# Joins between the stages of a two-layer decoder trunk: chunk before tile, projection copies between the steps of the norm, squares in PSUM

## What is computed

```
for i in range(2):
    x = x + (attention, retention)[i](rmsnorm(x, norm_mix[i]))
    a = rmsnorm(x, norm_ffn[i]) @ ffn_w_in[i];  gate, up = a[..., :2816], a[..., 2816:]
    x = x + (silu(conv(gate)) * up) @ ffn_w_out[i]
    x = x + sigmoid(rmsnorm(x, norm_pl[i]) @ pl_w_gate[i]) * (p[i] @ pl_w_proj[i])
return rmsnorm(x, norm_final)
```

## Time and profile before

| | |
|---|---|
| median of 3 runs | 1542.73 us (1542.4 to 1547.37) |
| profiled execution | 1548.81 us, of which the span of its instructions is 1547.0 |
| PE busy | 1514.2 us (98%), mean granted clock 0.993 |
| DVE, ACT, POOL busy | 777.3, 634.4, 822.8 us (50, 41, 53%) |
| DMA | 137.77 MB, mean 89 GB/s |

### The profile page before, as it was taken

The page is one execution under the profiler, slowest core; times in us unless marked ns, Lnnn a source line. Parts: engine busy times, 40 slices in busy tenths (PEclk is TensorE's granted clock), DMA queues, the critical chain, the costliest instruction groups (busy, mean ns, idle before and its releaser), DMA issues.

```text
span 1547.0 us, 20602 instructions
## 1 busy us (share of the span) xinstructions
PE 1514.2 (98%) x6874; PEld 1254.2 (81%) x6874; DVE 777.3 (50%) x1201; ACT 634.4 (41%) x955; POOL 822.8 (53%) x1014
## 2 busy tenths in 40 slices
PE   8999999999999999999999999999999999999996
PEld 5888887788888888887888888888788888888874
DVE  6898996555555411257343433423755555511155
ACT  6777875433323322244343423424533323322232
POOL 5343343766666655465445354453566666655551
PEclk9999999999999999999999999999999999999998
DMA  4111111222222322223222122221222222333221
GB/s 168 61 61 61 41 55 55 99 97 104 95 95 95 139 94 93 68 96 129 89 70 102 61 95 81 81 99 64 95 89 102 95 95 95 115 113 106 73 82 55
DMA packets 37192, 137.77 MB, mean 89 GB/s; under 512 B 4128, under 2 KB 4256, under 8 KB 37024
## 3 DMA queue, kind: packets, MB, share of 16 engines
q1 hardware_dynamic: 36576, 134.61, 25.0%
q10 hardware_dynamic: 576, 2.62, 0.5%
HBM read 135.12 MB, written 2.10 MB: 89 GB/s over the span
## 4 chain that ended last, share of the span: by engine, by line
PE 78%; issue 11%; POOL 7%; DVE 2%; ACT 0%; DMA 0%; DVEq 0%; POOLq 0%; SPq 0%; ACTq 0%
PE bank L339 24%; PE bank L343 24%; PE bank L342 24%; POOL wl L310 7%; PE bank L601 2%; PE bank L606 2%; PE bank L605 2%; DVE sumsq L723 0%; DVE xl L729 0%; PE bank L665 0%; DVE x L1094 0%; DMA raw<-in_w 0%; DVE sumsq_l L709 0%; DVE x L951 0%; DVE gated L948 0%
## 5 line engine op out<-in xcount | busy, mean ns | idle before, releaser
L310 POOL TENSOR_TENSOR wl<-raw,wh 128x256 fp32r<-128x256 f32 x1008 | 820.7, 846 | 690.8 <-ACT wh L1101 690.5
L339 PE MATMUL bank<-xh,wh 128*128 128x512 f32 x1280 | 503.7, 393 | 5.9 <-DVE xl L729 4.4
L342 PE MATMUL bank<-xl,wh 128*128 128x512 f32 x1280 | 500.4, 391 | 0.0
L343 PE MATMUL bank<-xh,wl 128*128 128x512 f32 x1280 | 500.4, 391 | 0.0
L1101 ACT ACTIVATE wh<-raw 128x1024 fp32r<-128x1024 f32 (+1 forms) x236 | 260.4, 1104 | 527.7 <-PE bank L339 470.4
L339 PEld LDWEIGHTS bank<-xh,wh 128*128 128x128 f32 x1280 | 241.6, 189 | 59.8 <-DVE xl L729 8.3
L343 PEld LDWEIGHTS bank<-xh,wl 128*128 128x128 f32 x1280 | 241.5, 189 | 51.0
L342 PEld LDWEIGHTS bank<-xl,wh 128*128 128x128 f32 x1280 | 241.7, 189 | 48.9
L743 DVE TENSOR_TENSOR x<-x,bank 128x512 f32<-128x512 f32 x56 | 38.4, 686 | 245.7 <-PE bank L343 245.6
L342 PE MATMUL bank<-yl,wh 128*128 128x512 f32 x352 | 137.0, 389 | 0.0
L343 PE MATMUL bank<-yh,wl 128*128 128x512 f32 x352 | 137.0, 389 | 0.0
(11 more groups left out here) (167 smaller groups left out, 1918.2 us busy)
## 6 DMA issues: line engine op xcount, KB each, us to landing
raw<-in_w SPq DMA_DIRECT2D x204, 512.0 KB, 3.2
raw<-in_w SPq DMA_DIRECT2D x32, 704.0 KB, 4.0
x<-in_xT SPq DMA_DIRECT2D x8, 256.0 KB, 5.8
outT<-x SPq DMA_DIRECT2D x8, 256.0 KB, 2.1
pin<-in_pT ACTq DMA_DIRECT2D x2, 512.0 KB, 3.3
decay<-in_consts ACTq DMA_DIRECT2D x1, 1024.0 KB, 5.6
rotary<-in_consts ACTq DMA_DIRECT2D x1, 512.0 KB, 3.5
cst<-in_consts SPq DMA_DIRECT2D x1, 256.0 KB, 7.5
```

The lines of the kernel that those rows point to most:

```text
L310: last = nc.gpsimd.tensor_tensor(wl[:, slot, cols], part[:, cols], wh[:, slot, cols].bitcast(F32), ALU.subtract)
L339: first = mm(out, ah_, bh_, start=start, stop=False, skip_group_check=True)
L342: mm(out, ah_, bl_, start=False, stop=False, skip_group_check=True)
L343: return mm(out, al_, bh_, start=False, stop=stop, skip_group_check=True)
```

## The change

Four edits. (1) The squares of x go into PSUM banks 5 and 7 instead of the SBUF buffers; the warm-up products write bank 6 instead of bank 7. (2) At the start ACT copies tile 2 behind square 3 instead of square 4, and DVE adds squares 2 and 3 ahead of the constants. (3) At the attention output and at the last retention head ACT runs chunk m ahead of the tile that stood in front of it; the wait for the first three chunks' products goes, since `x_chunk` waits for more. (4) DVE copies the projection chunks in `x_phase_before_embed`: chunk 0 to 3 between the last steps of the norm, 4 to 7 behind them.

```diff
-        rstd, ln_ms, square = sb("rstd", [T]), sb("ln_ms", [T]), sb("square", [2, T])
+        rstd, ln_ms = sb("rstd", [T]), sb("ln_ms", [T])
+        SQUARE = (bank[5], bank[7])
...
-                mm(O[1][:], rstd[:, 0:P], rstd[:], start=True, stop=True)
+                mm(O[0][:], rstd[:, 0:P], rstd[:], start=True, stop=True)
...
-                vec.tensor_tensor(sumsq[:], sumsq[:], square[:, par_, :], ALU.add).then_inc(sq_added, 1)
+                vec.tensor_tensor(sumsq[:], sumsq[:], SQUARE[par_][:], ALU.add).then_inc(sq_added, 1)
...
+            def take_proj(layer, m):
+                dve.wait_ge(chunk_done, C_PL[layer] + m + 1)
+                vec.tensor_copy(proj[:, m, :], bank[m % RING][:]).then_inc(chunk_freed, 1)
+
+            def x_phase_before_embed(layer, norm):
+
+                c0, last = C_FFNOUT[layer], KC - 1
+                norm_open(norm)
+                for k in range(KC):
+                    x_add(c0 + k, k % RING, k)
+                    if k:
+                        x_low_part(norm, k - 1)
+                        add_square(norm, k - 1, (k - 1) % 2)
+                take_proj(layer, 0)
+                x_low_part(norm, last)
+                take_proj(layer, 1)
+                add_square(norm, last, last % 2)
+                take_proj(layer, 2)
+                sum_high(norm)
+                take_proj(layer, 3)
+                sum_low(norm)
+                for m in range(RING, KC):
+                    take_proj(layer, m)
...
+            for k in range(2, 4):
+                add_square(0, k, k % 2)
             dve.wait_ge(cst_loaded, 16)
...
-            for k in range(2, KC):
+            for k in range(4, KC):
                 add_square(0, k, k % 2)
...
-                x_phase(C_FFNOUT[layer], norm + 1)
+                x_phase_before_embed(layer, norm + 1)
...
-                with dve.Fori(0, KC // RING) as i:
-                    for u in range(RING):
-                        m = RING * i + u
-                        dve.wait_ge(chunk_done, c0 + m + 1)
-                        vec.tensor_copy(one(proj, m), bank[u][:]).then_inc(chunk_freed, 1)
...
-                nc.scalar.activation(square[:, par_, :], one(x, k), ACT.Square).then_inc(x_squared, 1)
+                nc.scalar.activation(SQUARE[par_][:], one(x, k), ACT.Square).then_inc(x_squared, 1)
...
-                if k == 4:
+                if k == 3:
                     tile_high(2)
...
             for m in range(KC):
-                if m < RING - 1:
-                    act.wait_ge(chunk_done, C_ATTOUT + m + 1)
+                x_chunk(C_ATTOUT + m, 1, m, m % 2)
                 tile_high(N_ATTOUT + RING + m)
-                x_chunk(C_ATTOUT + m, 1, m, m % 2)
...
                 for m in range(KC):
+                    x_chunk(c + m, 4, m, m % 2)
                     if m % 2 == 0:
                         tile_high(n + RING + m // 2)
-                    x_chunk(c + m, 4, m, m % 2)
```

## The result

The changed kernel takes 1536.54 us (median of 6 runs, 1534.75 to 1536.6) against 1543.73 us for the kernel before beside it (6 runs, 1542.4 to 1547.37): a ratio of 0.9944, 95% interval 0.9929 to 0.9958. So it is faster by 0.56%, about 7 us, which is more than 0.3%. The prediction had the direction and the range (1526.0 to 1537.5), and its value, 1530.5, was 6 us too low. The profiled execution after has a span of 1534.8 us, 12.2 less than the span of 1547.0 before. Those 5 us between the two differences are what most of the experiments are about.

What follows compares the result with a forecast made beforehand. PE was taken to bound nearly everywhere, leaving gaps at joins and clock dips. Terms 2.2 + 3.2 + 3.1 + 1.0 + 1.3 = 10.8 us without clock; between 1531.9 and 1527.7 it took 1530.5 us, range 1526 to 1537.5.

Steps and rivals of the forecast that it cites:

- The squares in PSUM: Adding a square takes 0.69 us instead of 1225 ns beside POOL; ACT's square into a bank stays 0.62 us.
- The start: First sum of squares read 2.2 us earlier (1.5 to 2.2), and a clock dip of 1.7 us goes.
- the sum is read at 23.25: At the start, PE reads the sum at 23.25 us instead of 25.45, with constants taking 1.3 us.
- Attention output: Join into first MLP: 0.8 us lost at tile 4, 4.0 gained at the sum, net 3.2 without clock.
- The dip behind the gap: At tile 4 the gap grows to 2.4 us; the clock may fall, costing 1.7 us, held even.
- Projections: MLP to embedding, twice: PE's wait for the first projection bank goes, 2 x 1.55 = 3.1 us.
- Embedding to retention: Faster additions of squares bring the sum earlier: 1.0 us (0.7 to 1.2).
- Retention to MLP: Join into second MLP: sum read 1.3 us earlier (1.0 to 1.9), and a dip of 1.7 us goes.
- the first: Rival: squares in PSUM relieve nothing, 4.6 of 10.8 us lost, leaving 1536.5 us; chance 0.08.
- The second: Rival: at the attention output late tile loads put tile 10 before chunk 7, 1534.5 to 1537 us; chance 0.10.
- the fourth: Rival: ACT's write into a bank is slow, making the kernel slower, 1554 us at 2.5 us a square; chance 0.05.
- the third: Rival: no measurable change, from the first two rivals together or dips only changing place, 1538 to 1547 us; chance 0.08.

Runs made afterwards that it cites:

- edit 1 alone: Kernel before with only the squares in PSUM banks 5 and 7 and the warm-up in bank 6: 1535.78 us, ratio 0.994.
- the second profile: Kernel before, unchanged, run and profiled a second time: 1545.71 us, ratio 0.9994.

## Where the prediction held and where it failed

*The squares in PSUM*: right in size (0.69 predicted, 0.676 measured; POOL 813 ns). The square in a bank cost less than in SBUF, 580 against 615 ns, a side that my bounds left out. Of the larger fixed cost for a PSUM source in the table of the Trainium skill ("VectorE: DVE Perf Modes", section on the TRN2 errata) no run shows anything: 0.68 us with the operand in a bank, and the earlier trace rows has 677 ns as the shortest with both in SBUF.

*The start*: the largest miss. I gave it 2.2 us and a dip of 1.7; the first scores came 1.1 us earlier. The step that failed is "the sum is read at 23.25": it was 24.47, since the constants met POOL (1.97 us, not 1.3) and the dependent additions follow at 0.79 us, not 0.65. The dip was mis-sized as well: it had cost 0.1 us, being hidden behind `q_pack`. Edit 1 gave 1.2 to 1.3 us here and edit 2 took 0.4 back.

*Attention output*: the sum of the step was right, 3.2 us predicted and 262.70 - 259.43 = 3.3 measured without the dip. PE came back at tile 4 0.9 us later counted from the scores (I had 0.8), and from there to the sum it took 4.2 us less (I had 4.0). The reorder does that without edit 1 as well: with the squares in SBUF the same 4.2 us go. But edit 1 alone makes most of it unnecessary. With the old order it shortens the stretch by 1.5 us (first load early) or 2.9 (late), and on top of it the reorder costs 0.8 us in the first case and gains 0.3 in the second, with 1.6 lost where the clock dips. The two edits remove the same wait, so their gains don't add. What I missed is the consequence of my own term: a relieved POOL releases `raw` sooner, so tile 11 comes less late, and less is left for the reorder to get round. And that the 3.3 us came out is partly luck. Before's late load is in them: against the same orders with an early load (260.14) the change gains 0.7 us here.

*The dip behind the gap*, held even in the forecast, came in seven of ten executions (by their spans) and cost 1.6 us. The Trainium skill ("TensorE: Matmul & The Clock Gate", section "Why this matters for your kernels") warns only of longer idle gaps and would have had none; a gap of 2.32 us was enough, though not each time.

*Projections*: 3.1 predicted, 3.4 in the traces of before and after. In the order in which the edits stand, edit 1 has half of that. *Embedding to retention*: 1.0 predicted, 0.8 measured, all of it edit 1. *Retention to MLP*: 1.3 predicted, 1.95 measured (399.23 to 397.28), 1.1 of it by edit 1 and 0.8 by the reorder; and the dip there went (1.6).

*From the profile to the median*: between the two profiled executions 1.1 + 1.7 + 3.3 + 0.8 + 1.95 + 3.4 = 12.25 us went (start, the attention output with its new dip, each of the last four stretches with the dips that they lost). Less the two dips that counted and went, and with the one that came added back, it is 10.6, where the prediction had 10.8; the start's 1.1 us too much and the 0.9 too little at retention and the projections nearly cancel, which is luck. Yet the median moved 7.2 us. I took the 10.8 as what an execution without dips would gain. But the profiled execution of before also had a late load at the attention output, worth 2.5 us (262.70 against 260.14), and the change brings its own dip of 1.6 into most executions: 10.6 - 2.5 - 1.6 = 6.5. That before's quicker executions had an early first load is argued from their spans: 1541.1 us at the quickest, where the second profile less its one dip would give 1543.3. With early loads and no dip on either side the table gives 1.1 + 0.7 + 1.7 + 0.8 + 1.95 + 1.7 = 7.95 us, and the quickest executions of the two kernels beside each other, 1541.0 and 1533.2, are 7.8 apart.

Of the rivals, the first had a price of 1536.5 us, counted from 1531.9 and not from the forecast (1530.5 + 4.6 would be 1535.1); that the measured time is this number is chance. The second (late tiles in the ring of two) didn't happen: PE came back at 262.91 us and the sum had no wait. The first and the fourth were ruled out by 0.68 and 0.58 us. The dip that only changes its place, which I had listed under the third, is what happened at the attention output.

## What to carry to other kernels

Where two engines slow each other down on operands in SBUF, moving one operand to a free PSUM bank can be worth as much as all the reorderings together, and it changes what a reordering is worth: cost edits one on top of the other, in the order in which they act, not each against the old trace. Price a stall at the next point that all paths must pass; a dip inside a wait for another engine's chain cost 0.1 us here and not 1.7. And take a second profile of the kernel before ahead of pricing anything that comes after a load or with the clock: a dip is worth 1.6 us here, and came or not in executions of one program; a late load made 2.5 us between two profiles with the same orders in the stretch.

## What the hardware showed beyond that

A DVE operation on 128x128 took 0.74 to 0.78 us beside POOL and 0.21 us without it, a larger factor than that of the 128x512 additions (1.225 against 0.68 us). An ACT square of 128x512 is 35 ns shorter into PSUM (580) than into SBUF (615).

The clock's dips are not settled by the length of a gap. Behind 2.32 us at tile 4 it fell in seven of ten executions of the change by their spans, and not in the profiles of two variants with the same gap (2.31 and 2.32 us). Behind 1.35 us at 1118 us it fell in one profile of before and not in the other. Behind 1.73 us at the attention output's sum it fell, behind 1.74 at the start, with the squares in SBUF, it didn't. Behind a single gap of 1.06 us or less no profile shows a dip, but for the tail. What decides between two executions with the same gap stays open.
